# A recurrence with two state buffers, projections in pieces among its chunks, and the joins around it taken out, in a three-block transformer kernel in FP32

## What is computed

```python
# the delta rule, per head; c = 64 tokens in a chunk
t_inv = triangular_solve(eye + a, eye)      # a: strictly lower triangle
u = t_inv @ v_beta
w = t_inv @ (k_beta * exp(g))
qk = (qf @ kf.T) * decay
def chunk_step(state, (q_i, k_i, u_i, w_i, qk_i, g_i)):
    v_new = u_i - w_i @ state
    o_i = (q_i * exp(g_i)) @ state + qk_i @ v_new
    state = state * exp(g_last) + (k_i * exp(g_last - g_i)).T @ v_new
    return state, o_i
# the merge
y_dn = (rms_norm(o_dn) * dn_norm_g * silu(z_dn)) @ w_proj_dn
y_mb = (o_mb * silu(z_mb)) @ w_proj_mb
y = (sigmoid(m0) * y_dn + sigmoid(m1) * y_mb) @ w_out
```

## Time and profile before

| | |
|---|---|
| median of 3 runs | 2527.31 us (2527.21 to 2527.7) |
| the profiled execution, its span | 2532.4 us |
| PE busy | 2282.0 us, 90% of the span |
| DVE busy | 872.5 us, 34% |
| ACT busy | 417.4 us, 16% |
| DMA | 657.14 MB, 259 GB/s on average |

### The profile page before, as it was taken

One profiled execution on the slowest core, in us unless ns is written; L12 is line 12 of the kernel. 1 busy time (PEld: TensorE's weight loads), 2 busy tenths in 40 slices (PEclk: granted clock), 3 DMA queues, 4 the chain that ended last, 5 costly groups with the idle time before them and its releaser, 6 DMA issues. The chain is left out here.

```text
span 2532.4 us, 25068 instructions
## 1 busy us (share of the span) xinstructions
PE 2282.0 (90%) x9740; PEld 1316.8 (52%) x9740; DVE 872.5 (34%) x1800; ACT 417.4 (16%) x897; POOL 107.0 (4%) x74
## 2 busy tenths in 40 slices
PE   7998999988899898888779989898789999989998
PEld 4555343333333333333257677665558764647873
DVE  5675222212121111222246343644567301333201
ACT  1222111111101111111022211112321001222100
POOL 1000000000000000000000000000100000000000
PEclk8999999999999999999989998899999999989999
DMA  9767588999989999999977620575246543423441
GB/s 327 273 235 268 188 347 337 413 412 412 392 317 413 413 413 413 412 412 413 413 270 263 215 72 17 207 258 179 87 166 218 198 157 131 146 93 117 165 151 49
DMA packets 212413, 657.14 MB, mean 259 GB/s; under 512 B 8542, under 2 KB 13206, under 8 KB 195572
## 3 DMA queue, kind: packets, MB, share of 16 engines
q1 hardware_dynamic: 208528, 649.53, 67.4%
q0 software_dynamic: 1712, 3.60, 0.4%
q10 hardware_dynamic: 2004, 1.67, 0.2%
HBM read 653.72 MB, written 1.05 MB: 259 GB/s over the span
## 5 line engine op out<-in xcount | busy, mean ns | idle before, releaser
L1604 PE MATMUL ps<-w,XE 128*64 128x512 f32 x1152 | 336.8, 612 | 39.1 <-DMA w<-in_w_gate_up 27.4
L812 PE MATMUL ps<-HF,w 128*128 128x256 f32 x1408 | 311.9, 385 | 1.8 <-DVE CF L2914 1.8
L812 PEld LDWEIGHTS ps<-HF,w 128*128 128x128 f32 x1408 | 271.9, 193 | 42.3 <-issue 4.5
L1634 DVE TENSOR_TENSOR T<-ps,BB 128x512 f32<-128x512 f32 x64 | 44.2, 691 | 599.9 <-PE ps L1604 599.9
L1604 PEld LDWEIGHTS ps<-w,XE 128*64 128x64 f32 x1152 | 108.1, 141 | 200.7 <-issue 199.5
L1675 PE MATMUL ps<-w,AT 128*64 128x512 f32 x608 | 168.0, 604 | 23.5 <-DMA w<-in_w_down 16.8
L630 DVE SCALAR_TENSOR_TENSOR AUX<-w,CS,AUX 128x512 f32<-128x512 f32 (+1 forms) x228 | 169.8, 745 | 8.1
L812 PE MATMUL ps<-HT,w 128*128 128x256 f32 x640 | 149.6, 393 | 5.6 <-DVE dqk L2353 3.7
L828 PE MATMUL ps<-w,AF 128*128 128x512 f32 x352 | 151.6, 593 | 1.8 <-DVE AF L2936 1.8
L1604 PE MATMUL ps<-GR,XE 128*64 128x512 f32 x304 | 141.6, 621 | 11.2 <-DMA AUX<-in_w_gate_up 9.4
L828 PE MATMUL ps<-w,HT 128*128 128x512 f32 (+1 forms) x352 | 147.6, 573 | 0.3 <-DVE S L1449 0.3
(11 more groups left out here) (586 smaller groups left out, 2737.4 us busy)
## 6 DMA issues: line engine op xcount, KB each, us to landing
w<-in_w_gate_up SPq DMA_DIRECT2D x72, 2048.0 KB, 20.1
w<-in_w_down SPq DMA_DIRECT2D x38, 2048.0 KB, 20.5
w<-in_ada_w SPq DMA_DIRECT2D x24, 2048.0 KB, 8.0
w<-in_ffn_w_in SPq DMA_DIRECT2D x20, 2048.0 KB, 8.0
tables<-in_w_gate_up SPq DMA_DIRECT2D x19, 2048.0 KB, 21.7
GR<-in_w_gate_up SPq DMA_DIRECT2D x19, 2048.0 KB, 18.2
AUX<-in_w_gate_up SPq DMA_DIRECT2D x18, 2048.0 KB, 20.6
w<-in_w_in SPq DMA_DIRECT2D x17, 2048.0 KB, 9.5
```

The source lines that it names most:

```text
L812: ins = e.matmul(out_, w[:, k, c:c + n], HT[:, k, :], start=k == 0, stop=k == kc - 1, skip_group_check=True)
L1604: ins = e.matmul(b[j * n:j * n + n, :], FM.XE[:, side(x), 4 * kh + k, j * n:j * n + n], ring.tile(512, 1024, "gu", ex_, h, kh, x[0])[:, k, ...
L1634: e.tensor_tensor(FM.T1[:, :], bank(x, "gu", q), FM.BB[:, q * 512:q * 512 + 512], ADD).then_inc(*dve())
```

## The change

The join ahead of the inverse and the one behind the recurrence go, and with them the two waits of all engines. Piece by piece:

- The inverse's first step for t = 0 stands ahead of the attention on DVE; the steps 0 and 1 of one half stand together with an sg piece behind them on PE. The gating of the attention's output moves behind s = 3.
- `u` is computed once for both halves, at s = 13 (four products of 128 columns each), and evicted on ACT into `vb`.
- The recurrence computes only `w S`; DVE adds it to `u` (`wT` holds the negative). The first chunk, whose state is zero, has neither `w S` nor the product with `qg`. The state alternates between the two halves of `zm`.
- The attention's output is transposed at s = 9 (`turn_heads_pe`) and its projections (1 and 3) run as eight pieces of 8 records: one ahead of the recurrence, four among the chunks, three behind. `OT` now lies in `HT`.
- The modulation steps 24 to 26 move into the inverse and the recurrence, 27 behind it. The loads change to 1, 3, 0, 2.
- The sigmoids move into the inverse, in part into the evictions of the sg pieces. After the recurrence only the two delta projections remain in one piece.

```diff
-        f.OT, f.MX = sb("OT3", [128, 8, 256], c=ph), sb("MX", [128, 8, 256], c=ph)
+        f.OT, f.MX = f.HT, sb("MX", [128, 8, 256], c=ph)
...
-    S2 = F2.zm[:, 0, :]
+    S2 = [F2.zm[:, n % 2, :] for n in range(4)]
...
-        for hf in range(2):
-            for br, src in enumerate((T["w_proj_dn_2"][0], T["w_proj_mb_2"][0])):
-                ada_load(e, 24 + 2 * hf + br)
-                ring.load(e, src[:, 512 * hf:512 * hf + 512], 512, 512, "proj", 2 * hf + br)
+        for n, i in enumerate((1, 3, 0, 2)):
+            src = (T["w_proj_dn_2"][0], T["w_proj_mb_2"][0])[i % 2]
+            ada_load(e, 24 + n)
+            ring.load(e, src[:, 512 * (i // 2):512 * (i // 2) + 512], 512, 512, "proj", i)
...
-    def sg_piece_act(e, s):
+    def sg_piece_act(e, s, func=ACT.Copy):
...
             e.wait_ge(*at("sg", s - 1))
-            e.activation(SG[i // 2][:, i % 2, j, :], bank("sg", s - 1)[:, 0:256], ACT.Copy).then_inc(*act("sg", "out"))
+            e.activation(SG[i // 2][:, i % 2, j, :], bank("sg", s - 1)[:, 0:256], func).then_inc(*act("sg", "out"))
...
+    def turn_heads_pe(e, name, t, c0):
+        b = bank.take(e, name, t)
+        for k in range(4):
+            ins = e.transpose(b[:, cols(k)], F2.O[:, t, c0 + k * 128:c0 + k * 128 + 128], ident)
+        ins.then_inc(*pe(name, t))
...
+    def turn_heads_act(e, name, t, k0, scale=1.0):
+        e.wait_ge(*at(name, t))
+        e.activation(F2.OT[:, k0:k0 + 4, cols(t)], bank(name, t).rearrange("p (k q) -> p k q", k=4), ACT.Copy,
+                     scale=scale).then_inc(*act(name, "out"))
...
+    def proj_piece_pe(e, i, j):
...
+        b = bank.take(e, "proj piece", i, j)
+        feat_pe(e, b[:, 0:256], ring.tile(512, 512, "proj", i), j * 128, 128, F2.OT[:, 4:8, :]).then_inc(*pe("proj piece", i, j))
...
+    def proj_piece_dve(e, i, j):
+        e.wait_ge(*at("proj piece", i, j))
+        to = SG[i // 2][:, 1, j, :]
+        e.tensor_tensor(to, bank("proj piece", i, j)[:, 0:256], to, MUL).then_inc(*dve())
+        dve.leave("bank", "proj piece", i, j)
...
+            b = bank.take(e, "du", t)
+            by_heads_pe(e, b, lambda hd: p.U[:, HC[hd]], lambda hd: p.vb[:, HC[hd]]).then_inc(*pe("du", t))
...
+            e.wait_ge(*at("du", t))
+            e.activation(p.vb[:, :], bank("du", t), ACT.Copy).then_inc(*act("u", t))
+            act.leave("bank", "du", t)
...
+    def new_state_pe(e, n):
...
+        t, rw = n // 2, slice(64 * (n % 2), 64 * (n % 2) + 64)
+        p = F2.per[t]
+        v = p.vn if n else p.vb
+        e.wait_ge(*(at("vn", n) if n else at("u", 0)))
+        b = bank.take(e, "dS", n)
+        by_heads_pe(e, b, lambda hd: p.kg[rw, HC[hd]], lambda hd: v[rw, HC[hd]]).then_inc(*pe("dS", n))
...
+    def by_state_pe(e, n):
...
+        e.wait_ge(*at("wT", t))
+        e.wait_ge(*at("S2", n))
+        b = bank.take(e, "dn", n)
+        for hd in range(4):
+            ins = e.matmul(b[rw, HC[hd]], p.wT[:, hd * 128 + c0:hd * 128 + c0 + 64], S2[n][:, HC[hd]], start=True, stop=True,
+                           skip_group_check=True)
...
+    def chunk_out_pe(e, n):
...
+        v = p.vn if n else p.vb
...
+        if n:
+            e.wait_ge(*at("vn", n))
...
+        for hd in range(4):
+            cc = slice(hd * 128 + c0, hd * 128 + c0 + 64)
+            if n:
+                e.matmul(bo[rw, HC[hd]], p.qg[:, cc], S2[n][:, HC[hd]], start=True, stop=False, skip_group_check=True)
+            ins = e.matmul(bo[rw, HC[hd]], p.qk[rw, cc], v[rw, HC[hd]], start=n == 0, stop=True, skip_group_check=True)
+        ins.then_inc(*pe("do", n))
...
+    def recurrence_pe(e):
+        new_state_pe(e, 0)
+        chunk_out_pe(e, 0)
+        proj_piece_pe(e, 1, 1)
+        by_state_pe(e, 1)
+        proj_piece_pe(e, 1, 2)
+        new_state_pe(e, 1)
+        chunk_out_pe(e, 1)
+        by_state_pe(e, 2)
+        proj_piece_pe(e, 1, 3)
+        new_state_pe(e, 2)
+        chunk_out_pe(e, 2)
+        by_state_pe(e, 3)
+        proj_piece_pe(e, 3, 0)
+        chunk_out_pe(e, 3)
...
-        end(pe, "pe", "second b")
-        join(e, "second b")
-        for s in range(14):
+        ada_sum_pe(e, 23)
+        for t in range(2):
+            inverse_pe(e, t, 0)
+            inverse_pe(e, t, 1)
+            sg_piece_pe(e, 10 + t)
...
-                e.matmul(b[rw, HC[hd]], p.U[:, cc], p.vb[:, HC[hd]], start=True, stop=False, skip_group_check=True)
-                ins = e.matmul(b[rw, HC[hd]], p.wT[:, cc], S2[:, HC[hd]], start=False, stop=True, skip_group_check=True)
...
-        end(pe, "pe", "second c")
-        join(e, "second c")
-        turn_pe(e, "OT2", lambda t, k: F2.O[:, t, cols(k)], 8)
-        features(e, "OT2")
-        for i in range(4):
-            ada_sum_pe(e, 23 + i)
-            feats_pe(e, ("proj", i), ("proj", i), ring.tile(512, 512, "proj", i), 4,
-                     F2.OT[:, 4 * (i % 2):4 * (i % 2) + 4, :])
+            if s == 8:
+                ada_sum_pe(e, 24)
+            if s == 9:
+                e.wait_ge(*at("att2", "gated"))
+                for t in range(2):
+                    turn_heads_pe(e, "att2 turned", t, 512)
+            if s == 10:
+                ada_sum_pe(e, 25)
+        e.wait_ge(*at("att2 turned", "out"))
+        proj_piece_pe(e, 1, 0)
+        recurrence_pe(e)
+        ada_sum_pe(e, 26)
+        proj_piece_pe(e, 3, 1)
+        e.wait_ge(*at(("hn2", 0), "out"))
+        turn_heads_pe(e, "heads2 turned", 0, 0)
+        proj_piece_pe(e, 3, 2)
+        proj_piece_pe(e, 3, 3)
+        e.wait_ge(*at(("hn2", 1), "out"))
+        turn_heads_pe(e, "heads2 turned", 1, 0)
+        e.wait_ge(*at("heads2 turned", "out"))
+        for i in (0, 2):
+            feats_pe(e, ("proj", i), ("proj", i), ring.tile(512, 512, "proj", i), 4, F2.OT[:, 0:4, :])
...
-        end(act, "act", "second b")
-        join(e, "second b")
-        for s in range(14):
+        sg_piece_act(e, 10)
+        for t in range(2):
+            inverse_act(e, t, 1)
+            sg_piece_act(e, 11 + t, (ACT.Copy, ACT.Sigmoid)[t])
...
-            e.activation(F2.per[t].vn[rw, :], bank("dn", n)[rw, :], ACT.Copy).then_inc(*act("vn", n))
...
-        for hf in range(2):
-            for br in range(2):
-                e.activation(SG[hf][:, br, :, :], SG[hf][:, br, :, :], ACT.Sigmoid).then_inc(*act("merge", hf))
+            sg_piece_act(e, 11 + s, ACT.Sigmoid)
+            if s in (5, 7, 11):
+                merge_act(e, *{5: (0, 1, 4), 7: (0, 0, 4), 11: (1, 0, 3)}[s])
+            if s == 9:
+                for t in range(2):
+                    turn_heads_act(e, "att2 turned", t, 4)
...
+    def headnorm2_dve(e, t):
+        headnorm_dve(e, ("hn2", t), bank("do", t), 4, SQ2[:, 0:512], st[:, 44 + 4 * t:48 + 4 * t], F2.zd[:, t, :],
+                     F2.O[:, t, 0:512], left=("do", t))
...
+    def state_dve(e, n):
...
+        if n == 0:
+            e.tensor_copy(S2[1], bank("dS", 0)).then_inc(*dve("S2", 1))
+        else:
+            c = 64 * (n % 2) + 63
+            for hd in range(4):
+                e.scalar_tensor_tensor(out=S2[n + 1][:, HC[hd]], in0=S2[n][:, HC[hd]],
+                                       scalar=F2.per[n // 2].eR[:, hd * 128 + c:hd * 128 + c + 1],
+                                       in1=bank("dS", n)[:, HC[hd]], op0=MUL, op1=ADD).then_inc(*dve("S2", n + 1))
...
+    def new_values_dve(e, n):
...
+        e.tensor_tensor(p.vn[rw, :], p.vb[rw, :], bank("dn", n)[rw, :], ADD).then_inc(*dve("vn", n))
...
+    def recurrence_dve(e):
+        proj_piece_dve(e, 1, 0)
+        ada_acc_dve(e, 26, range(2))
+        state_dve(e, 0)
+        proj_piece_dve(e, 1, 1)
+        ada_acc_dve(e, 26, range(2, 3))
+        new_values_dve(e, 1)
+        ada_acc_dve(e, 26, range(3, 4))
+        state_dve(e, 1)
+        proj_piece_dve(e, 1, 2)
+        ada_acc_dve(e, 26, range(4, 5))
+        new_values_dve(e, 2)
+        ada_acc_dve(e, 26, range(5, 6))
+        state_dve(e, 2)
+        proj_piece_dve(e, 1, 3)
+        ada_acc_dve(e, 26, range(6, 7))
+        new_values_dve(e, 3)
+        ada_acc_dve(e, 26, range(7, 8))
...
+        inverse_dve(e, 0, 0)
...
-        own(e, dve)
-        for t in range(2):
-            e.tensor_tensor(F2.O[:, t, 512:1024], F2.O[:, t, 512:1024], F2.zm[:, t, :], MUL).then_inc(*dve())
-        end(dve, "dve", "second b")
-        join(e, "second b")
-        for s in range(14):
+        inverse_dve(e, 1, 0)
+        ada_put_dve(e, 23)
+        for t in range(2):
+            inverse_dve(e, t, 1)
+            inverse_dve(e, t, 2)
...
+            if s == 3:
+                for t in range(2):
+                    e.tensor_tensor(F2.O[:, t, 512:1024], F2.O[:, t, 512:1024], F2.zm[:, t, :], MUL).then_inc(*dve("att2", "gated"))
+                ada_acc_dve(e, 24)
+            if s == 5:
+                ada_acc_dve(e, 25)
+            if s == 9:
+                ada_put_dve(e, 24)
+            if s == 11:
+                ada_put_dve(e, 25)
+        e.wait_ge(*at("merge"))
+        recurrence_dve(e)
```

(13 more changed lines are left out.)

109 lines of the change are left out of this document (45 added, 64 removed).

## The result

The median fell from 2527.26 us (2524.6 to 2527.7) to **2489.49 us** (2485.4 to 2491.0), four runs of each: 37.8 us less, a ratio of 0.986 with a 95% interval of 0.9837 to 0.9883. Forecast were 2495.6 and a range of 2487 to 2512.

A forecast was written before the change was run, and what follows sets the result against it. PE, busy 90% of the span, was taken as the bound through its idle and low-clock times. Four legs, -3.2 + 7.3 - 16.8 - 19.0 = -31.7, took 2527.3 to 2495.6 us, range 2487 to 2512.

The forecast's parts named there:

- Leg 3: Recurrence, up to the last chunk: 40.6 us becomes 23.8 with waits gone and full clock, 16.8 gained; bounds 10 to 18.
- rule on tiling modes: Recurrence: changing tiling mode drains the engine; 0.13 us per change, about ten changes, gain 1.3 us smaller, 2496.9.
- about 5: Recurrence: of the 16.8 us gained, about 5 are waits, 3.6 products gone, the rest clock, less four pieces moved in.
- Leg 4: Last chunk to output projection: 47.7 us becomes 28.7, 19.0 gained; bounds 14 and 21.
- after such a wait: Last chunk to output projection: the first remaining projection priced at 8.75 us because it follows a wait, the second at 7.0.
- Leg 2: Ladder, to the recurrence: PE gets 7.3 us more work; DVE's two accumulations fit in its waits, costing nothing.
- I leave the slow sg piece as it is: The sg piece behind step 2 stays at 6.5 us, where full clock gives half, since PE still idles before it.
- Leg 1: Attention's last product to the sg piece behind step 2: 3.2 us gained, DVE setting the border; bounds 0 and 6.
- the recurrence stayed fast: Rival denied here: clock stays low in the recurrence, 18 us more; 2514 if all low, 2505 if half; chance 0.13.
- nothing was given back: Rival denied here: third block's loads bound what follows, so PE waits as much as it comes early; 2525, chance 0.03.
- DVE as the bound: Rival: with 19 us of accumulations moved earlier, PE waits for DVE in ladder and recurrence; 8 us back, 2504, chance 0.12.
- the load as the bound: Rival: output weights land after 13.2 us instead of 7.8 behind a modulation load, 3 us lost; 2499, chance 0.04.

The follow-up runs named there:

- filled kernel: Kernel before the change, plus seven groups of 16 idle products where PE waited in the recurrence: median 2520.5 us against 2525.5 on the same chip.
- second profile: The changed kernel run once more, unaltered, on a later chip: median 2495.1 us, 30.5 below the kernel before the change on that chip.
- the start: Changed kernel with the ladder's first transposes and products ahead of the attention's last two sg pieces, and two DVE operations earlier: median 2486.0 us.
- the sums put back: Changed kernel with DVE's accumulations of modulation chunks 24 to 26 and their PE sums put back between the merge's projections: median 2517.7 us.
- start and end: Changed kernel with PE's early ladder products moved ahead, DVE's second-half norm earlier and the output projection begun on its ready blocks: median 2482.0 us.
- load first: Changed kernel with both the earlier ladder products and earlier norm and output projection, plus output weights loaded ahead of the modulation chunk: median 2477.8 us.

## Why the prediction was right, point by point

**Leg 3**, the heart of it, was forecast at 23.8 and took 23.7. What no row had shown at full clock, the product with the state, was taken as 1.1 between 1.0 and 2.07; the trace has 1.09 from its start to that of the next product:

```profile
1549.92 1.16 PE L2277 MATMUL ps<-dvb,dkg 64*128 64x128 f32 x8
1551.01 1.08 PE L2454 MATMUL ps<-dvb,dqk 64*64 64x128 f32 x8
1552.02 1.99 PE L812 MATMUL ps<-HT,w 128*128 128x256 f32 x8
1553.94 1.09 PE L2433 MATMUL ps<-zm,dT 128*64 128x128 f32 x8
```

The output of a chunk took 2.9, not 3.0, that of chunk 0 1.0, not 1.3, and a piece 1.92 from start to start here against 1.82 at the end of the ladder (1548.10 to 1549.92). That last 0.1 is what the rule on tiling modes of the Trainium skill ("TensorEngine Tiling (Array Packing)", "Tiling Modes") was weighed for: the trace agrees with it in kind. The size was put too high: four pieces make 0.4 us of it, not the 1.3 of the ten changes, and the terms taken too high in the sum hid it. The clock stayed at 1.00, and with the filled kernel before it is shown, not only argued, that the 64-column products don't hold it down once PE has no waits. The split of the gain that the step gives, "about 5" of waits and 3.6 of products, doesn't hold: PE stood idle for 7.6 of the 40.6 us; the real products took 33.0 at the granted clock of 0.66 and about 22 in the filled kernel, so 11 are the clock; without its pieces the changed recurrence has 16.0 of work, so 6 are products gone; and 7.7 of pieces came in. 7.6 + 11 + 6 - 7.7 is the 16.9 measured. The sum of 23.8 doesn't use that split, so it wasn't hurt. The pieces alone, taken out again, cost 7 us, and the new products 2.6. That the rest comes from fewer hand-overs between the engines is argued; no run takes it by itself.

**Leg 4** was 19.0 forecast, 20.6 measured, for a cause that isn't mine: the first projections took 14.1 us and not 15.8 as "after such a wait"; in the second profile they took 15.8, and the leg 28.4 for the 28.7 forecast. The two pairs of waits came as followed (1.38 and 0.78, 2.2 together, for 2.4; 2.11 for 2.4), and the load was there. What the step lacked is the account of DVE: it says what PE does, and its sum would have been the same had DVE kept the accumulations, which cost 27 us with the loads that they hold up.

**Leg 2** is the term that was mis-sized: +7.3 forecast, +3.1 measured. 2.9 us of the difference is the sg piece (3.69 for 6.54), "I leave the slow sg piece as it is": it is slow in most runs, but not in this one, and in the second profile leg 2 was +5.8. The other 1.3 are prices taken from slow rows. The transposes were halved from the 3.65 of the earlier trace rows, which ran at the low clock; eight records took 0.87 from start to start. The two sums took 0.81 each for 0.9:

```profile
1535.28 1.04 PE L2227 MATMUL ps<-tables,O 128*128 128x128 f32 x8
...
1539.72 0.95 PE L650 MATMUL ps<-tables,AUX 128*128 128x1 f32 x8
1540.54 2.03 PE L2277 MATMUL ps<-dT,XN 128*128 128x128 f32 x16
```

DVE's accumulations were hidden, as forecast. The first used its spare time up (DVE went on to `dT` without a wait), but PE didn't wait; of the second 1.06 us of DVE's wait were left where "1" was forecast, and the cover behind it measured 2.9.

**Leg 1** was -3.2 forecast and -2.9 measured, after a wait for `qk` of t = 1 as followed through, with DVE's wait for the transposes at 1.19 for "some 1.2"; putting the join and the first step back gave 3.2 back. That DVE sets the border was right for this order of the work; that it had to be so was wrong by 5 us, as the start showed.

**The total** is 6 us better than forecast. The four legs came out 5.6 better: 4.2 in leg 2, 1.6 in leg 4, 0.3 worse in leg 1. Of that 4.5 are the clock at the sg piece and at the first projections, which the later profile doesn't have; its four legs are 33.3 shorter than before, for 31.7 forecast, and its median is 2495.1. That 5.6 in the legs and 6 in the median agree is luck: between them lie 1.5 lost in the output projection and 7.9 of the profile outside the stretch, and there two profiles of the changed kernel differ from each other by 3.2 ahead of it and 6.0 behind it. On the later chip the changed kernel lies 30.5 below the one before, for 31.7 forecast; with single runs of the kernel before between 2513 and 2536, no median here confirms the forecast to better than a few us, and the prediction's 0.2% for what a measurement tells apart was too fine. None of the rivals came: the recurrence stayed fast, DVE and the loads were in time, nothing was given back. But two of them were near. DVE as the bound is what the sums put back show, and the load as the bound appears as soon as 4 us more are gained.

## What to carry to other kernels

A chain of small products between engines costs twice, by its waits and by the clock that they bring down, so independent work of PE set into such waits can be free or better than free; look for it in what follows, and price it at full clock. When work of one engine is moved out of a stage, move the other engines' work and the buffers that it holds with it, or the stage stays as long as it was. Before an engine's chain is called the bound, see which small products of the waiting engine stand in its queue behind large ones; and after each wait won, look at which load is next, and which slot it has to wait for.

## What the runs showed of the hardware that was not expected

- The clock's price can exceed the work that avoids it: 14.4 us of useless products in 40.6 made the stretch 37.1 us, at a granted clock of 1.00 instead of 0.66.
- In the recurrence without pieces the clock fell (0.77 granted) with PE busy 20.3 of 22.7 us and no wait over 0.78; in the kernel before it was 0.66 with no wait over 1.31 inside the recurrence.
- The same code has different clocks in different executions: the sg piece behind a wait took 3.7 to 6.5 us in seven profiles. Where PE's last wait ahead of it was one of 0.6 us, two groups of transposes earlier, it took 3.62 in all three profiles (start, start and end, load first).
